# Query and key halves copied by transfers, stick-breaking sums over summed later blocks, bias rows on GpSimd, in a two-layer hybrid trunk

## Chip, cores and metric

One core of a Trainium2 chip runs the whole kernel in one launch. The metric is the device time in microseconds of one execution.

## What is computed

Input x is 512 tokens of 1024 values, float32. Each of 2 layers has a SwiGLU feed-forward part (inner width 2816), a mixer of three causal attention branches, and a second feed-forward part; a last norm closes. The mixer, shortened from the reference:

```python
u = _rmsnorm(h, mix_norm[l])
z = u @ w_in[l]
(a_q, a_k, a_v, b_q, b_k, b_v, b_f, c_q, c_k, c_v, g) = jnp.split(z, split_idx, axis=-1)
...
# branch A: softmax(q k + ALiBi), two of them, p[0] - lam * p[1]; 4 heads of 2 x 64
# branch B: softmax(q k + c_q - c_k), c = cumsum(log_sigmoid(forget)); 8 heads of 64
# branch C, stick-breaking, 8 heads of 64:
z = jnp.einsum('bqhd,bkhd->bhqk', qb, k).astype(f32) * scale
log_keep = jnp.where(strict, jax.nn.log_sigmoid(-z), 0.0)
later = lax.cumsum(log_keep, axis=3, reverse=True) - log_keep
w = jnp.where(strict, jnp.exp(jax.nn.log_sigmoid(z) + later), 0.0)
...
m = (gates[:, :, 0] * (o_a @ proj_a[l]) + gates[:, :, 1] * (o_b @ proj_b[l]) + gates[:, :, 2] * (o_c @ proj_c[l]))
h = h + m @ w_out[l]
```

What matters below is `later`: for each key, the sum of the log factors over all keys that come after it.

## The kernel before

Everything is kept transposed: features on the 128 partitions, the 512 tokens along the row. Products run in a rounded 32-bit format. To keep float32 accuracy a value is held as two parts, a high part (ACT rounds, helper `hi`, line 755) and a low part (DVE subtracts, helper `lo`, line 1098), and a product is three matmuls (`three`, lines 372 to 374): high x high, high x low, low x high.

**Weights** come as a stream of units: one unit is 128 x 1024 values, eight blocks, 512 KB. SyncE (SP) loads unit n + 3 into the slot of unit n as soon as DVE has made unit n's low part (`w_set`); three slots. `split(k)` on ACT and on DVE makes the two parts of slot k. One unit through PE is 24 matmuls of 512 columns (`u_unit`).

**The head tiles.** In the mixer a layer has 4 tiles, each with 128 columns of every branch: two heads of B, two of C, one of A (with its two softmaxes). One tile takes 9 units of w_in (`HEAD_UNITS`): q, k, v for C, then B, then A. Unit n's product lies in PSUM bank n mod 2; DVE takes it (`take`, line 1208), scaled by the norm, to `tile(n % 2)` and counts `staged`. PE works through a written-out order (`heads` and `rest_of_tile`): between blocks of units (`unit(4, 0, 3)` is blocks 0 to 2 of unit 4) it puts scores, transposes (`turn_values`, `turn_probs`), sums and weighted products of the heads, so that ACT and DVE have time to prepare them. ACT and DVE have their own written-out orders for the same work; each engine runs strictly in its order and waits on semaphores. `rest_of_tile` finishes branch A of the tile before, while the units of the next one begin. The first tile of a layer also has the forget gate (`forget`) in it.

**Query and key halves.** A q or k unit holds two heads, 64 partitions each. `qk_hi` on ACT writes rounded halves where the score matmuls want them: q of each head twice (`q_twice`), k once (`k_both`), and for branches A and B once more (`k_bias`), each from the half in `tile`: 4, 2 or 4 operations of 64 x 512. `qk_lo` on DVE writes the low halves: 2 of 64 x 512. The other halves of `q_rest` hold bias rows (`rows`, DVE, line 1228), 4 in a tile, that select the head's forget or ALiBi bias from `bias_l`.

**Stick-breaking.** The 4 key blocks of 128 keys have their own PSUM banks (`SB0 + j`), with the queries from block j on: 512, 384, 256 and 128 columns. `stick_scores` fills them, block 0 first. ACT makes log(1 + exp(-|z|)) in three operations for each block (`stick_logs`), DVE completes it (`stick_softplus`), and both split it into parts in `PT_HI` and `PT_LO`. `stick_sums` then adds to bank j a triangular product of block j and a product with a matrix of -1 for each later block i:

```python
for i in range(NQ):
    pe.wait_ge(pt_set, c.next(pt_set))
    n, *parts = wide_keys(i)
    for j in range(i + 1):
```

`wide_keys` gives at least 256 columns; for block 3, zeros stand beside its 128. The banks are then exponentiated (`stick_exp`), split (`stick_hi`, `stick_lo`) and multiplied with the values (`weighted(2, hd)`), which waits for the low part of one block after the other.

## Time and profile before

| | |
|---|---|
| median of 3 runs | 2586.7 us (2586.26 to 2587.92) |
| the profiled execution | 2585.08 us, its span 2583.3 us |
| PE busy | 2554.5 us, 99% |
| DVE busy | 1429.1 us, 55% |
| ACT busy | 1119.4 us, 43% |
| granted clock of PE, mean | 0.998 |
| one head tile | 76.9 us, 8 of them |
| moved by DMA | 238 MB, mean 92 GB/s |

All times are microseconds from the span's start. PE, ACT, DVE, POOL (GpSimd) and SP (SyncE) are the engines. L372 is line 372 of the kernel. Matmuls are pipelined and their ends are modelled, so the pitch of their starts tells more than their duration. An idle time in a row stands in brackets with the work that ended it.

### The profile page before, as it was taken

The numbers are of one execution on the slowest core, as the hardware profiler recorded it, in microseconds if no ns is written. First come the engines' busy times: TensorE is split into PE (matmuls) and PEld (weight loads), VectorE is DVE, ScalarE is ACT, GpSimd is POOL, SyncE is SP. The second block draws the span as 40 slices with busy tenths as digits, with TensorE's granted clock in tenths as the row PEclk, the third lists the DMA queues.
The fourth block names the chain that finished last, engine by engine and source line by source line (L and its number), as shares of the span: only waits on it lengthen the run. The fifth ranks groups of instructions, "written<-read, shape, count | busy, mean of one in ns | idle before, by whom it ended". The sixth has DMA issues, their size and how long they took to land.

```text
span 2583.3 us, 36860 instructions
## 1 busy us (share of the span) xinstructions
PE 2554.5 (99%) x11838; PEld 2124.9 (82%) x11838; DVE 1429.1 (55%) x2164; ACT 1119.4 (43%) x1888; POOL 3.5 (0%) x12
## 2 busy tenths in 40 slices
PE   7999999999999999999999999999999999999997
PEld 6888888888888888888888888888888888888886
DVE  5444347888854454444344443488888455544434
ACT  4223237777732242232232222478776223422322
POOL 0000000000000000000000000000000000000000
PEclk9999999999999999999999999999999999999999
DMA  4222332111222232223332223221212322322233
GB/s 168 97 97 95 101 106 66 59 66 58 66 95 94 88 123 98 97 94 102 106 107 97 97 94 102 97 67 58 66 58 66 103 93 96 115 97 96 94 104 105
DMA packets 65767, 238.05 MB, mean 92 GB/s; under 512 B 7296, under 2 KB 7552, under 8 KB 65408
## 3 DMA queue, kind: packets, MB, share of 16 engines
q1 hardware_dynamic: 65664, 236.79, 27.6%
q8 instruction: 52, 0.85, 0.1%
q14 instruction: 51, 0.42, 0.1%
HBM read 234.66 MB, written 2.10 MB: 92 GB/s over the span
## 4 chain that ended last, share of the span: by engine, by line
PE 97%; DVE 1%; issue 1%; ACT 0%; DMA 0%; DVEq 0%; ACTq 0%; SPq 0%
PE ps L372 30%; PE ps L374 30%; PE ps L373 30%; PE ps L529 2%; PE ps L460 1%; PE ps L449 1%; PE ps L503 1%; PE ps L502 1%; PE ps L451 1%; PE ps L516 0%; PE ps L466 0%; PE ps L518 0%; DVE scratch L1114 0%; PE ps L445 0%; PE ps L536 0%
## 5 line engine op out<-in xcount | busy, mean ns | idle before, releaser
L755 ACT ACTIVATE w_hi<-w_raw 128x1024 fp32r<-128x1024 f32 x441 | 468.4, 1062 | 1164.2 <-PE ps L374 1163.4
L372 PE MATMUL ps<-u_hi,w_hi 128*128 128x512 f32 x2368 | 929.1, 392 | 11.3 <-DVE w_lo L1098 11.3
L374 PE MATMUL ps<-u_hi,w_lo 128*128 128x512 f32 x2368 | 922.9, 390 | 0.0
L373 PE MATMUL ps<-u_lo,w_hi 128*128 128x512 f32 x2368 | 922.7, 390 | 0.0
L1098 DVE TENSOR_TENSOR w_lo<-w_raw,w_hi 128x1024 fp32r<-128x1024 f32 x441 | 538.2, 1222 | 313.3 <-ACT w_hi L755 305.8
L372 PEld LDWEIGHTS ps<-u_hi,w_hi 128*128 128x128 f32 x2368 | 445.4, 188 | 103.2 <-issue 12.3
L374 PEld LDWEIGHTS ps<-u_hi,w_lo 128*128 128x128 f32 x2368 | 445.1, 188 | 93.8
L373 PEld LDWEIGHTS ps<-u_lo,w_hi 128*128 128x128 f32 x2368 | 445.4, 188 | 90.8 <-issue 1.2
L372 PE MATMUL ps<-area,w_hi 128*128 128x512 f32 x1024 | 398.8, 389 | 0.4 <-DVE h L1118 0.4
L374 PE MATMUL ps<-area,w_lo 128*128 128x512 f32 x1024 | 398.4, 389 | 0.0
L373 PE MATMUL ps<-area,w_hi 128*128 128x512 f32 x1024 | 398.4, 389 | 0.0
L755 ACT ACTIVATE area<-scratch 64x512 fp32r<-64x512 f32 (+5 forms) x426 | 235.4, 583 | 123.7 <-DVE scratch L1449 64.0
L1098 DVE TENSOR_TENSOR area<-scratch,area 128x512 f32 (+5 forms) x336 | 199.2, 611 | 56.0 <-ACT area L755 53.1
L372 PEld LDWEIGHTS ps<-area,w_hi 128*128 128x128 f32 x1024 | 192.2, 188 | 42.1 <-issue 2.5
L374 PEld LDWEIGHTS ps<-area,w_lo 128*128 128x128 f32 x1024 | 192.2, 188 | 40.0
L373 PEld LDWEIGHTS ps<-area,w_hi 128*128 128x128 f32 x1024 | 192.2, 188 | 39.9
L1132 DVE TENSOR_TENSOR scratch<-ps,rstd 128x512 f32<-128x512 f32 x88 | 60.9, 692 | 257.0 <-PE ps L374 257.0
L1128 DVE TENSOR_TENSOR scratch<-ps,rstd 128x512 f32<-128x512 f32 x88 | 60.9, 692 | 187.4 <-PE ps L374 179.0
L1430 DVE TENSOR_TENSOR scratch<-ps,rstd 128x512 f32<-128x512 f32 x48 | 33.0, 690 | 100.6 <-PE ps L374 100.4
L845 ACT ACTIVATE scratch<-ps,stat 128x128 f32<-128x128 f32 (+3 forms) x128 | 66.2, 524 | 34.3 <-DVE stat L1233 34.3
L1108 DVE SCALAR_TENSOR_TENSOR u_lo<-h,par,u_hi (+1 forms) x56 | 41.6, 751 | 63.7 <-ACT u_hi L767 63.7
L1118 DVE SCALAR_TENSOR_TENSOR h<-ps,h 128x512 f32 (+1 forms) x48 | 33.1, 691 | 67.9 <-PE ps L374 67.9
(118 smaller groups left out, 1563.2 us busy)
## 6 DMA issues: line engine op xcount, KB each, us to landing
w_raw<-weights SPq DMA_DIRECT2D x441, 512.0 KB, 3.3
h<-x SPq DMA_DIRECT2D x2, 1024.0 KB, 6.7
out<-scratch SPq DMA_DIRECT2D x8, 256.0 KB, 2.2
scratch<-const_b SPq DMA_DIRECT2D x1, 512.0 KB, 10.5
scratch<-const_r SPq DMA_DIRECT2D x1, 320.0 KB, 9.7
scratch<-lambdas SPq DMA_DIRECT2D x1, 256.0 KB, 10.7
cst<-const SPq DMA_DIRECT2D x1, 137.0 KB, 3.1
par<-params SPq DMA_DIRECT2D x1, 94.0 KB, 2.1
```

What stands on the lines that cost most here:

```text
L372: pe.matmul(dst, hi, x_hi, start=start, stop=False, **kw)
L373: pe.matmul(dst, hi, x_lo, start=False, stop=False, **kw)
L374: return pe.matmul(dst, lo, x_hi, start=False, stop=stop, **kw)
L529: last = pe.matmul(ps[:, SB0 + j, width - n:width], negtri_r if i == j else negones_r, part, start=False, stop=i == NQ - 1, skip_group_che ...
L755: return act.activation(dst, src, ACT.Copy)
L845: act.activation(query_block(buf, i), ps[:, SB0 + i, 0:(i + 1) * P], ACT.Exp, bias=neg_max(buf, i), accum_out=total(buf, i)).then_inc(exp_ ...
L1098: return dve.tensor_tensor(dst, src, hi_part.bitcast(F32), ALU.subtract)
L1108: dve.scalar_tensor_tensor(u_lo[:, bass.ds(at, SEQ)], h[:, bass.ds(at, SEQ)], times(gain), u_hi[:, bass.ds(at, SEQ)].bitcast(F32), ALU.mul ...
L1118: dve.scalar_tensor_tensor(h[:, bass.ds(at, SEQ)], ps[:, bank, :], factor, h[:, bass.ds(at, SEQ)], ALU.mult, ALU.add).then_inc(h_set, 1)
L1128: dve.tensor_tensor(a, ps[:, 2 * pair, :], rstd[:], ALU.mult).then_inc(gate_in, 1)
L1132: dve.tensor_tensor(b, ps[:, 2 * pair + 1, :], rstd[:], ALU.mult).then_inc(up_set, 1)
L1430: dve.tensor_tensor(tile(6 * (k % 2)), ps[:, k, :], rstd[:], ALU.mult).then_inc(tail_read, 1)
```

## The change

Six things change together, all in the mixer.

1. **Transfers copy the halves.** `qk_hi` becomes one rounding of 128 x 512 into one new tile `rounded`, and `qk_lo` one subtraction in place in `tile(k % 2)`. SP issues transfers of 64 x 512 (128 KB) from there to `q_twice`, `k_both`, `k_bias` and `q_rest`: 22 for high parts and 12 for low parts in a tile. They stand in SP's one queue between the weight loads, in a written-out order (`tile_loads`). ACT may round the next one only when the last high parts have landed and DVE has read `rounded`; `take` may overwrite `tile(k % 2)` only when its low parts have landed; the first scores of a branch wait for all of it (`wait_qk`).
2. **Sums over summed blocks.** Key blocks are scored and worked on in the order 3, 2, 1, 0. DVE adds block 3 to block 2 and the result to block 1 (`later_sum`), the sums are split (`later_hi`, `later_lo`) into a new area, and `stick_sums` has 14 matmuls for 20. Each bank counts `stick_set` when it is complete, so ACT may exponentiate bank 3 first. `weighted(2, hd)` waits for all four blocks.
3. **Bias rows on GpSimd.** The four `rows` of a tile run there, let go by the fourth take of the tile.
4. **Base rows** of the bias are loaded again in each layer, in float32, straight into `bias_l` and `tile(6)`; the copies at the start go away, and so do four tiles (`o_rest`, `o_whole`, `base_l`, `base_r`). `o_whole` is now `tile(7)`. In the first tile of a layer, both bias tiles are finished ahead of the take of k.
5. **PE's order** is shifted by one to three blocks at most places: values and probabilities are turned earlier, the sums of both heads start one block later.
6. **The orders of ACT and DVE** are rewritten to fit.

```diff
+            def move_hi(branch, which):
+
+                sp.wait_ge(qk_hi_set, counts.next(qk_hi_set))
+                for hd in range(2):
+                    src = rounded[half(hd), :].bitcast(F32)
+                    if which == 0:
+                        sp.dma_start(q_twice(branch, hd)[half(hd), :].bitcast(F32), src).then_inc(hi_moved, 16)
+                        sp.dma_start(q_twice(branch, hd)[half(1 - hd), :].bitcast(F32), src).then_inc(hi_moved, 16)
+                    else:
+                        sp.dma_start(k_both(branch, hd)[half(hd), :].bitcast(F32), src).then_inc(hi_moved, 16)
+                        if branch != 2:
+                            sp.dma_start(k_bias(branch, hd)[half(hd), :].bitcast(F32), src).then_inc(hi_moved, 16)
+
+            def move_lo(branch, which, k):
+
+                sp.wait_ge(qk_lo_set, counts.next(qk_lo_set))
+                for hd in range(2):
+                    src = tile(k % 2)[half(hd), :]
+                    dst = q_rest(branch, hd)[half(hd), :] if which == 0 else k_both(branch, hd)[half(1 - hd), :]
+                    sp.dma_start(dst.bitcast(F32), src).then_inc(lo_moved[k % 2], 16)
+
+            def tile_loads(base):
+
+                load_next(base, 0)
+                move_hi(2, 0)
+                move_lo(2, 0, 0)
+                move_hi(2, 1)
+                move_lo(2, 1, 1)
+                load_next(base + 1, 1)
+                load_next(base + 2, 2)
+                move_hi(1, 0)
+                move_lo(1, 0, 3)
+                load_next(base + 3, 0)
+                move_lo(1, 1, 4)
+                move_hi(1, 1)
+                load_next(base + 4, 1)
+                load_next(base + 5, 2)
+                load_next(base + 6, 0)
+                move_hi(0, 0)
+                move_lo(0, 0, 6)
+                move_lo(0, 1, 7)
+                move_hi(0, 1)
+                load_next(base + 7, 1)
+                load_next(base + 8, 2)
+
...
+                def rows(head, branch, hd):
+                    o = half(1 - hd)
+                    pool.tensor_scalar(q_rest(branch, hd)[o, :], bias_l[o, :], cst[o, C_SEL + head:C_SEL + head + 1], None,
+                                       ALU.mult).then_inc(rows_set, 1)
+
+                pool.wait_ge(bias_set, layer + 1)
+                for t in range(NT):
+
+                    pool.wait_ge(staged, (layer * NT + t) * HEAD_UNITS + 4)
+                    rows(2 * t, 1, 0)
+                    rows(2 * t + 1, 1, 1)
+                    rows(t + N_FOX, 0, 0)
+                    rows(t + N_FOX, 0, 1)
...
+            def wait_qk(branch):
+
+
+                pe.wait_ge(hi_moved, c.next(hi_moved, 16 * (6 if branch == 2 else 8)))
+                for k in range(2):
+                    pe.wait_ge(lo_moved[k], c.next(lo_moved[k], 16 * 2))
...
+                if branch == 2:
+                    pe.wait_ge(pt_set, c.next(pt_set, NQ))
                 for j in range(NQ):
-                    pe.wait_ge(pt_set, c.next(pt_set))
+                    if branch != 2:
+                        pe.wait_ge(pt_set, c.next(pt_set))
...
-                for j in range(NQ):
+                for j in reversed(range(NQ)):
...
             def stick_sums():
 
-                for i in range(NQ):
+                def add(j, matrix, parts, m, stop):
+                    n = max(WIDE, (NQ - j) * P)
+                    for k, part in enumerate(parts):
+                        last = pe.matmul(ps[:, SB0 + j, n - m:n], matrix, part, start=False, stop=stop and k == 1,
+                                         skip_group_check=True)
+                    return last
+
+                def own(j, stop):
                     pe.wait_ge(pt_set, c.next(pt_set))
-                    n, *parts = wide_keys(i)
-                    for j in range(i + 1):
-                        width = max(WIDE, (NQ - j) * P)
-                        for part in parts:
-                            last = pe.matmul(ps[:, SB0 + j, width - n:width], negtri_r if i == j else negones_r,
-                                             part, start=False, stop=i == NQ - 1, skip_group_check=True)
-                        if i == NQ - 1:
-                            last.then_inc(stick_set, 1)
+                    n, *parts = wide_keys(j)
+                    return add(j, negtri_r, parts, n, stop)
+
+                def all_later(j, stop):
+                    pe.wait_ge(pt_set, c.next(pt_set))
+                    parts = later(LATER_HI, j), later(LATER_LO, j)
+                    return add(j, negones_r, parts, (NQ - 1 - j) * P, stop)
+
+
+
+                own(3, True).then_inc(stick_set, 1)
+                own(2, False)
+                n, *parts = wide_keys(3)
+                add(2, negones_r, parts, n, True).then_inc(stick_set, 1)
+                own(1, False)
+                all_later(1, True).then_inc(stick_set, 1)
+                all_later(0, False)
+                own(0, True).then_inc(stick_set, 1)
...
             def heads(before):
 
                 if before:
                     rest_of_tile(unit)
-                    unit(2)
+                    unit(2, 0, 5)
                     turn_probs(0)
-                    unit(3, 0, 3)
+                    unit(2, 5)
                     weighted_whole()
-                    unit(3, 3, 5)
+                    unit(3, 0, 4)
                     diff_norm()
+                    unit(3, 4, 5)
                 else:
                     unit(0, first=True, before=False)
                     sum_of_squares()
@@ -582,26 +705,25 @@
                 unit(4, 0, 3)
                 if before:
                     pe.wait_ge(o_rstd, c.next(o_rstd))
-                unit(4, 3, 6)
                 turn_values(0)
+                unit(4, 3, 7)
                 stick_sums()
-                unit(4, 6)
+                unit(4, 7)
                 unit(5, 0, 4)
                 weighted(2, 0, before)
                 stick_scores(1)
                 unit(5, 4)
-                unit(6, 0, 7)
+                unit(6)
                 stick_sums()
-                unit(6, 7)
-                unit(7, 0, 4)
+                unit(7, 0, 2)
+                turn_values(1)
+                unit(7, 2, 4)
                 weighted(2, 1)
                 scores(1, 0)
-                unit(7, 4, 5)
-                turn_values(1)
-                unit(7, 5)
-                unit(8, 0, 1)
+                unit(7, 4)
+                unit(8, 0, 2)
                 turn_probs(0)
-                unit(8, 1)
+                unit(8, 2)
                 weighted(1, 0)
                 scores(1, 1)
                 c.skip(exp_set, 2 * NQ)
...
             def qk_hi(branch, which, k, takes=1):
                 act.wait_ge(staged, c.next(staged, takes))
-                for hd in range(2):
-                    src = tile(k % 2)[half(hd), :]
-                    if which == 0:
-                        hi(q_twice(branch, hd)[half(1 - hd), :], src)
-                        last = hi(q_twice(branch, hd)[half(hd), :], src)
-                    else:
-                        last = hi(k_both(branch, hd)[half(hd), :], src)
-                        if branch != 2:
-                            last = hi(k_bias(branch, hd)[half(hd), :], src)
-                last.then_inc(qk_hi_set, 1)
+
+                act.wait_ge(hi_moved, c.value(hi_moved))
+                act.wait_ge(qk_lo_set, c.value(qk_lo_set))
+                hi(rounded[:], tile(k % 2)).then_inc(qk_hi_set, 1)
+                c.skip(hi_moved, 16 * (2 if branch == 2 and which else 4))
+                c.skip(qk_lo_set)
...
+            def later_hi(j):
+                act.wait_ge(later_sum_set, c.next(later_sum_set))
+                hi(later(LATER_HI, j), key_block(1, j + 1)).then_inc(pt_hi_set, 1)
...
+                softplus_hi(3)
+                softplus_hi(2)
+                softplus_hi(1)
+                values_hi(2)
+                later_hi(1)
+                split(0)
+                later_hi(0)
                 softplus_hi(0)
-                softplus_hi(1)
-                softplus_hi(2)
-                split(0)
-                softplus_hi(3)
-                values_hi(2)
+                stick_exp(3)
+                stick_exp(2)
                 if before:
                     output_hi(0, t - 1)
+                stick_exp(1)
                 stick_exp(0)
-                stick_exp(1)
-                stick_exp(2)
-                stick_exp(3)
+                stick_hi(3)
+                stick_hi(2)
+                stick_hi(1)
                 stick_hi(0)
                 split(1)
-                stick_hi(1)
-                stick_hi(2)
-                stick_hi(3)
                 qk_hi(1, 0, 3, 2)
+                output_rest(0)
                 stick_logs(0)
...
+                dve.wait_ge(base_landed, layer * 32 + 32)
+                dve.scalar_tensor_tensor(bias_l[:], run_hi, mask(0), bias_l[:], ALU.mult, ALU.add).then_inc(vec_done, 1)
                 dve.wait_ge(vec_done, c.next(vec_done))
-                dve.scalar_tensor_tensor(bias_l[:], soft, mask(1), bias_l[:], ALU.mult, ALU.add).then_inc(vec_done, 1)
+                dve.scalar_tensor_tensor(bias_l[:], soft, mask(1), bias_l[:], ALU.mult, ALU.add).then_inc(bias_set, 1)
+                dve.scalar_tensor_tensor(right, run_hi, mask(2), right, ALU.mult, ALU.add).then_inc(vec_done, 1)
                 dve.wait_ge(vec_done, c.next(vec_done))
-                stage(1, 1.0)
-                dve.scalar_tensor_tensor(neg, run_hi, mask(2), base_r[:], ALU.mult, ALU.add).then_inc(vec_done, 1)
-                dve.wait_ge(vec_done, c.next(vec_done))
-                dve.scalar_tensor_tensor(neg, soft, mask(3), neg, ALU.mult, ALU.add).then_inc(forget_in, 1)
-                c.skip(forget_in)
-
-            def stage(k, scale):
-                take(k, scale)
-                split(k % SLOTS)
+                dve.scalar_tensor_tensor(right, soft, mask(3), right, ALU.mult, ALU.add).then_inc(forget_in, 1)
+                take(1, 1.0)
+                split(1)
...
             def take(k, scale):
 
-                if k >= 2:
-                    dve.wait_ge(qk_set, c.peek(qk_set, 0))
+
+                dve.wait_ge(lo_moved[k % 2], c.value(lo_moved[k % 2]))
                 dve.wait_ge(unit_done, c.next(unit_done))
                 dve.scalar_tensor_tensor(tile(k % 2), ps[:, k % 2, :], scale, rstd[:], ALU.mult, ALU.mult
                                          ).then_inc(staged, 1)
 
-            def stage_qk(branch, which, k):
-                stage(k, SCALE if which == 0 else 1.0)
-                qk_lo(branch, which, k)
-
             def qk_lo(branch, which, k):
                 dve.wait_ge(qk_hi_set, c.next(qk_hi_set))
-                for hd in range(2):
-                    src = tile(k % 2)[half(hd), :]
-                    if which == 0:
-                        last = lo(q_rest(branch, hd)[half(hd), :], src, q_twice(branch, hd)[half(hd), :])
-                    else:
-                        last = lo(k_both(branch, hd)[half(1 - hd), :], src, k_both(branch, hd)[half(hd), :])
-                last.then_inc(qk_set, 1)
-                c.skip(qk_set)
-
-            def rows(head, branch, hd):
-                o = half(1 - hd)
-                dve.tensor_scalar(q_rest(branch, hd)[o, :], bias_l[o, :], cst[o, bass.ds(head + C_SEL, 1)], None,
-                                  ALU.mult).then_inc(rows_set, 1)
+                lo(tile(k % 2).bitcast(F32R), tile(k % 2), rounded[:]).then_inc(qk_lo_set, 1)
+                c.skip(lo_moved[k % 2], 16 * 2)
...
+            def later_sum(j):
+
+                k = key_block(1, j + 1)[:, P:]
+
+                dve.wait_ge(pt_set, c.value(pt_set))
+                dve.tensor_tensor(k, k, key_block(1, j + 2), ALU.add).then_inc(later_sum_set, 1)
+
+            def later_lo(j):
+                dve.wait_ge(pt_hi_set, c.next(pt_hi_set))
+                lo(later(LATER_LO, j), key_block(1, j + 1), later(LATER_HI, j)).then_inc(pt_set, 1)
...
+                stick_softplus(3)
+                take(3, SCALE)
+                stick_softplus(2)
+                stick_softplus(1)
                 stick_softplus(0)
-                stick_softplus(1)
-                stick_softplus(2)
-                stick_softplus(3)
+                softplus_lo(3)
+                softplus_lo(2)
+                later_sum(1)
+                softplus_lo(1)
+                later_lo(1)
+                later_sum(0)
+                later_lo(0)
                 softplus_lo(0)
-                softplus_lo(1)
-                softplus_lo(2)
-                softplus_lo(3)
                 if before:
                     output_lo(0, t - 1, layer)
-                take(3, SCALE)
                 values_lo(2)
+                stick_lo(3)
+                stick_lo(2)
+                stick_lo(1)
                 stick_lo(0)
+                take(4, 1.0)
+                qk_lo(1, 0, 3)
+                split(0)
+                output_whole(0)
+                split(1)
+                stick_softplus(3)
+                stick_softplus(2)
+                stick_softplus(1)
+                stick_softplus(0)
+                softplus_lo(3)
+                softplus_lo(2)
+                later_sum(1)
+                softplus_lo(1)
...
```

## Rows read from the trace of the kernel before

**Rows 1.** the page: its span and the busy time of the engines.
```profile
span 2583.3 us, 36860 instructions
...
PE 2554.5 (99%) x11838; PEld 2124.9 (82%) x11838; DVE 1429.1 (55%) x2164; ACT 1119.4 (43%) x1888; POOL 3.5 (0%) x12
```

**Rows 2.** waits of PE over the span: total us, times, longest.
```profile
PE ps L372 <- DVE w_lo L1098: 11.3, 2, 10.7
PE ps L393 <- DVE scratch L1114: 6.8, 2, 3.5
```

**Rows 3.** a stage of the trace, one tile: busy us and count by engine.
```profile
504.00:581.00 77.00, 77.00 (x418) 65.89 (x417) 64.48 (x136) 60.46 (x139) 0.00 (x0) 1.00 0.19 63
```

**Rows 4.** timeline of PE, pitch of matmuls by width: start us, us.
```profile
497.05 0.39 PE L502 MATMUL ps<-area,v_area 128*128 128x512 f32 x1
497.28 0.39 PE L503 MATMUL ps<-area,v_area 128*128 128x512 f32 x1
497.51 0.33 PE L502 MATMUL ps<-area,v_area 128*128 128x384 f32 x1
...
497.85 0.28 PE L502 MATMUL ps<-area,v_area 128*128 128x256 f32 x1
497.97 0.28 PE L503 MATMUL ps<-area,v_area 128*128 128x256 f32 x1
```

**Rows 5.** timeline of PE in the tile of 529 to 606.
```profile
558.90 0.39 PE L512 MATMUL ps<-cst_b 128*128 128x128 bf16 x4
...
560.47 0.40 PE L372 MATMUL ps<-u_hi,w_hi 128*128 128x512 f32 x1
...
566.97 3.06 PE L529 MATMUL ps<-area,cst_r 128*128 128x512 f32 x20
569.87 0.40 PE L372 MATMUL ps<-u_hi,w_hi 128*128 128x512 f32 x1
...
573.97 0.39 PE L502 MATMUL ps<-area,v_area 128*128 128x512 f32 x1
```

**Rows 6.** ACT by form, 504 to 581: busy, mean ns.
```profile
L755 ACT ACTIVATE area<-scratch 64x512 fp32r<-64x512 f32 x22 | 13.4, 627 | 0.3
```

**Rows 7.** DVE by form, 504 to 581: busy, mean ns.
```profile
L1098 DVE TENSOR_TENSOR area<-scratch,area 64x512 fp32r<-64x512 f32 x12 | 8.2, 686 | 0.5 <-ACT area L755 0.3
...
L1228 DVE TENSOR_SCALAR area<-bias_l,cst 64x512 fp32r<-64x512 f32 x4 | 1.9, 481 | 0.1
```

**Rows 8.** timeline of ACT in that tile, logarithms and roundings.
```profile
560.37 0.96 ACT L857 ACTIVATE scratch<-ps 128x512 f32<-128x512 f32 x2
...
564.52 1.36 ACT L755 ACTIVATE area<-scratch 128x512 fp32r<-128x512 f32 x3
```

**Rows 9.** timeline of DVE in that tile.
```profile
549.93 0.75 DVE L1253 SCALAR_TENSOR_TENSOR scratch<-scratch,stat 128x512 f32<-128x512 f32 x1
...
555.08 2.79 DVE L1098 TENSOR_TENSOR area<-scratch,area 64x512 fp32r<-64x512 f32 x4
...
565.19 1.50 DVE L1098 TENSOR_TENSOR area<-scratch,area 128x512 fp32r<-128x512 f32 x3
...
567.26 0.75 DVE L1291 SCALAR_TENSOR_TENSOR scratch<-ps,lam,scratch 128x512 f32<-128x512 f32 x1
```

**Rows 10.** DMA issues on SP's queue at the start: start us, us.
```profile
4.85 0.45 SPq L334 DMA_DIRECT2D scratch<-const_b  x1
```

**Rows 11.** DMA issues by line: KB each, us to landing.
```profile
w_raw<-weights SPq DMA_DIRECT2D x441, 512.0 KB, 3.3
...
out<-scratch SPq DMA_DIRECT2D x8, 256.0 KB, 2.2
```

**Rows 12.** timeline of PE and DVE in the first tile of layer 0.
```profile
401.52 0.75 DVE L1196 SCALAR_TENSOR_TENSOR scratch<-scratch,cst 128x512 f32<-128x512 f32 x1
...
405.05 0.40 PE L512 MATMUL ps<-cst_b 128*128 128x128 bf16 x4
```

**Rows 13.** one source line on POOL: ns min/median/max.
```profile
L355 POOL MEMSET area<- x2: 521/524/526, 391.0 to 1666.4; 64x512 f32 x2
```

247 lines of the change are left out of this document (137 added, 110 removed).

## The prediction

> **What bounds the kernel now.** I read the page first: TensorE (PE) is busy for 2554.5 of 2583.3 us, VectorE (DVE) for 1429, ScalarE (ACT) for 1119 [rows 1]. A busy PE can still be a waiting PE, so the next view is the waits of PE: 11.3 and 6.8 us, in two places each, at the start and around the norms, and nothing in the mixer [rows 2]. The stage view of one head tile (77 us) says the same: PE 77.00, DVE 64.5, ACT 60.5 [rows 3]. So inside a tile PE never starves, and only two things can move the time: matmul work that goes away, and a wait that appears. Work taken from ACT and DVE is worth nothing by itself; it buys slack. The last view is the timeline of PE, for the price of a matmul: 512 columns start 0.23 us apart (0.227 over long runs), 384 columns 0.17, 256 columns 0.12 [rows 4].
>
> **The matmuls that go.** `stick_sums` runs 16 times (2 layers, 4 tiles, 2 heads). Before, key block i goes through the matrix unit once for each block j <= i, in a high and a low part: 2 matmuls of 512 columns, 4 of 384, 6 and 8 of 256. By the pitches that is 2 x 0.23 + 4 x 0.17 + 14 x 0.12 = 2.82 us; the trace has 2.90 from the first of the 20 to the next matmul, the changeover from the transposes included [rows 5]. After: own blocks 3, 2, 1, 0 (256, 256, 384, 512 columns), block 3 into bank 2 (256), the summed blocks into bank 1 (256) and bank 0 (384), each twice: 8 of 256, 4 of 384, 2 of 512, 2.10 us. Six of 256 columns are gone: 6 x 0.118 = 0.71 us, 16 times: **11.3 us**. No other matmul changes its shape or count; the moved transposes and blocks are the same ones in another order, so I price the move at nothing on PE itself. What can hold it back are the operands.
>
> **Work off PE.** Per tile ACT drops 22 half-tile roundings of 627 ns (13.4 us) [rows 6] and gains 6 full ones of about 0.64 and 4 of the summed blocks (0.4 to 0.5 each): some 7.8 us less. DVE drops 12 half-tile subtractions of 686 ns and 4 bias rows of 481 ns [rows 7], gains 6 subtractions of 0.69 and 8 small ones for the sums: some 3 us less. PE hides both engines, so they are worth 0. Dropped with them is one 512 KB constant at the start, behind the loads that matter: 0.
>
> **The first sum of a tile, followed step by step.** Times are those of the profiled tile. The first-head scores start at 558.90 and end at 560.47, the sums start at 566.97 [rows 5]. ACT takes 4.15 us from the first absolute value to the first rounding (560.37 to 564.52) [rows 8]. In the new order the norm of branch A is 0.68 us (three matmuls) earlier and block 3, the narrow one, is scored first, so ACT starts at about 559.7 and rounds from 563.8. Then comes a ladder between DVE and ACT that was not there: round blocks 3, 2, 1; their low parts; sum of 2 and 3 (ready 565.7); ACT rounds it to 566.2; its low part 566.65; sum with block 1 at 567.1; ACT rounds it (384 columns) to 567.65 and block 0 to 568.2; low part of block 0 ready at 568.95. The durations of the steps are those of the same widths: 1.50 us for low parts of 512, 384 and 256 columns together [rows 9], 1.36 for the roundings [rows 8]. The 1.06 us rounding of weights in the middle is under the ladder's DVE steps. PE starts the sums one block later, at 567.65, and reaches block 0 last, 12 matmuls or 1.64 us on: 569.3. Slack 0.35 us: no wait, but little to spare. The second head has no such squeeze: PE puts 36 matmuls (8.2 us) there, and I find 1.4 us of slack.
>
> **The weighted product behind it** now waits for all four blocks at once, since they come in the order 3 to 0. Sums end 569.75, 15 matmuls later PE is there: 573.2 (573.97 before, [rows 5]). DVE from the low part of block 0, at pitches of 0.6 to 0.65 [rows 9]: output of branch A (0.65), ACT rounds it (0.7), its low part (0.6), values (0.7), low parts of 3, 2, 1 (0.95) and 0 (0.7): 573.3. I charge 0.15 us in the 6 tiles that have a tile before: **+0.9**.
>
> **The transfers.** SP takes 0.45 us for one issue [rows 10], and a transfer lands 2.2 us (256 KB out) to 3.3 us (512 KB weights) after it [rows 11]. The line through the two gives 1.65 us for the 128 KB of a half; nothing in the trace copies SBUF to SBUF, so I bound it by 1.65 and 3.3 and take 2.2, the nearest row. The Trainium skill (DMA: Bandwidth & Descriptors, Anatomy of one DMA) gives some 2.0 us plus bytes by 436 GB/s, 2.3 us here, for another issue path; by that the sum would be the same. The tight place is branch C's keys. The last difference and the take of k's unit end at 550.68 now [rows 9]; the scores in front of them come three matmuls (0.68 us) earlier, so 550.0, in the other order. ACT rounds q by 550.6; four issues, the last started at 551.9 and landed at 554.1. Today DVE starts on q's low part at 555.08 [rows 9]; the transposes ahead of it move up by 9 matmuls (2.0 us), the 1.2 us of a weight remainder is in the way, and I put its end at 554.0. Only after both may ACT round k: 554.8. Two issues for its high parts, two for the low parts, the last started at 556.2, landed at 558.4. The scores start at 558.90: no wait. In the first tile of a layer the left and right bias come ahead of k; the bias ends about where it does now, 402.27, k's low part at 402.7, the last issue starts at 403.15 and lands at 405.35, and PE is there at 405.05 [rows 12]: 0.3 us, twice: **+0.6**. On SP the weight loads stand behind these waits: the load behind branch B's moves comes some 10 us later than its slot is free, but lands (3.3 us) some 7 us before its rounding. The others have more. Transfers of the other branches have 1 us or more to spare; they are used a head later.
>
> **Bias rows on GpSimd.** Four 64x512 products per tile, let go by the fourth take, at about 563.5. DVE does one in 0.48 us [rows 7]; on GpSimd the trace has only a fill of that shape, 0.52 us [rows 13], as the lower end; as the upper, 1.1 us, twice it. They end between 565.7 and 568, and nobody needs them before 590. But from 564.75 DVE is on the ladder. If the two engines get in each other's way, DVE is late by d, and the product behind the ladder by nearly all of it (6 tiles), the sums of the first tiles by d less 0.35. No row shows them together; below, d = 0; above, each of the last two or three GpSimd operations holds DVE for its length, d = 2 or more. I take d = 0.3, half of one operation, since a DVE operation there is short and half the rows are done by then: 6 x 0.3 = **+1.8**.
>
> The Trainium skill (SBUF, Who interferes with whom) says a DVE instruction with two SBUF inputs and a GpSimd one that reads SBUF exclude each other for the whole instruction. No trace here shows it. It is rival B.
>
> **Sum.** -11.3 + 0.9 + 0.6 + 1.8 = -8.0 us. The profiled execution took 2585.08 us (span 2583.3), 1.6 under the median of the runs; its span would become 2575.3, and the median 2586.7 - 8.0 = **2578.7 us**.
>
> **Rivals.**
> - A, the above, 50%. Its own range: 2575.4 with no wait at all, to 2581.5.
> - B, GpSimd holds DVE, 25%. For: the rows start 1.2 us ahead of the ladder and last at least 2.1. Against: the last two-input operations of DVE may fit between. With d = 1.2: -11.3 + 1.5 + 6 x 1.2 + 2 x 0.85 = -0.9, **2585.8**. Up to d = 0.65 it stays faster by 0.2%.
> - C, the transfers are late, 20%; this is the one that ends slower. The chain holds two landings in a row, since q and k share one rounded tile. With a landing of L us the last one is at 553.98 + 2L in the 6 later tiles, and at 403.15 + L in the 2 first. L = 3.3, as weights take: 1.7 x 6 + 1.4 x 2 = 13 in place of A's 0.6: +4.4, **2591**. It costs the gain from L = 2.6, and makes the kernel slower by 0.2% from 3.4; at L = 4, some **2601**. For: 64-partition copies are not in the trace, and issues of 0.45 us follow each other. Against: 256 KB took 2.2.
> - D, the sums give nothing, because a wait that PE's modelled ends hide sits there already: 5%, **2586.7**. Against: the 20 matmuls run at the pitch of their widths.
>
> **Chances.** A change of 0.2% (5.2 us) is about what a measurement of this kernel can tell from none. Faster: all of A and parts of B and C (d up to 0.65, L up to 2.6): 0.60. Same: the middle of B and C, and D: 0.24. Slower: C from L = 3.4, B from d = 2.0: 0.16. The range reaches from no waits and a little more, 2574.5, to near C's 2591, 2590, with some 5% left out below and 13% above.
>
> **What would show it.** In the profile after: 14 matmuls per sum, 2.1 us from the first to the next, and PE without named waits except about 0.3 us at the first scores of a layer. B shows as two-input DVE operations in the ladder longer than 0.69 us or starting late while POOL is busy, and a wait of PE for the low parts of the first head. C shows as PE waiting for a DMA at the branch C scores, and as a time to landing above 2.6 us. I am wrong if the tile does not get 1.42 us shorter but for these waits, or if a wait shows in the second head or in branches A and B, whose chains I found loose.

## The result

The changed kernel takes 2595.75 us (median of 7 runs, 2594.02 to 2598.28); the kernel before took 2586.7 us beside it (7 runs, 2585.55 to 2587.92). The ratio is 1.0035, 95% interval 1.0023 to 1.0046: slower by 9 us, where I had predicted 8 us faster and a range that ended at 2590.0. The profiled execution took 2594.02 us.

The page of the changed kernel, to be read beside [rows 1]:

```profile
span 2592.2 us, 37391 instructions
...
PE 2551.0 (98%) x11742; PEld 2111.8 (81%) x11742; DVE 1414.4 (55%) x2146; ACT 1055.3 (41%) x1792; POOL 56.8 (2%) x44
```

TensorE is busy for 3.5 us less, ACT for 64 and DVE for 15 less, and the span is 8.9 us longer: work went and waits came. The waits of PE name them (engine, output, line of the waiting instruction, what it waited for: total us, times, longest):

```profile
PE ps L467 <- DVE w_lo L1236: 13.0, 2, 10.7
PE ps L488 <- DVE scratch L1252: 5.9, 2, 3.5
PE ps L617 <- DMA area<-scratch: 3.9, 8, 0.7
PE ps L631 <- DVE area L1236: 3.9, 8, 0.5
PE ps L547 <- DMA area<-rounded: 1.7, 7, 0.3
PE ps L607 <- DVE area L1236: 1.3, 6, 0.2
PE ps L467 <- issue: 0.8, 1, 0.8
```

The first two are those of [rows 2]. The next four are new, once for each tile or nearly: branch C's scores (L617) and B's (L547) wait for a transfer, the first sums of a tile (L631) and the weighted product behind them (L607) for DVE. The last is a single stop at 1297.7, where layer 1 begins. The named part of such a wait is less than what PE loses, since the ends of matmuls are modelled; the loss is the gap less the pitch of a matmul. The timeline of PE in one tile (start us, busy us, engine, line) shows both kinds:

```profile
482.72 0.40 PE L469 MATMUL ps<-u_hi,w_lo 128*128 128x512 f32 x1
483.83 0.40 PE L617 MATMUL ps<-cst_b 128*128 128x128 bf16 x4 [0.71 <-DMA area<-scratch]
...
492.73 1.88 PE L631 MATMUL ps<-area,cst_r 128*128 128x256 f32 x12
495.09 0.73 PE L631 MATMUL ps<-area,cst_r 128*128 128x512 f32 x2 [0.48 <-DVE area L1236]
495.65 0.39 PE L467 MATMUL ps<-u_hi,w_hi 128*128 128x512 f32 x1
...
498.83 0.39 PE L469 MATMUL ps<-u_hi,w_lo 128*128 128x512 f32 x1
499.44 0.50 PE L607 MATMUL ps<-area,v_area 128*128 128x512 f32 x1 [0.22 <-DVE area L1236]
```

The 14 matmuls of the first sums last from 492.73 to 495.65, 2.92 us, against 2.90 for the 20 of before [rows 5]; the second head's last 2.10 against 2.81. So the shorter sums are there, and the first ones lose all of it to one wait, for the low part of block 0. From the start of one tile's first sums to the next it is 77.9 us (492.73 to 570.62), against 76.92 before (490.05 to 566.97). By the same view of both kernels, piece by piece: first sums +0.02, second -0.71, C's scores +0.5, the product behind the sums +0.5, B's scores +0.4, and +0.2 at changeovers from transposes to matmuls, of which a tile has one or two more; +0.9 of the 1.0. Both layers show it alike. Outside the mixer one place differs: where layer 1 begins, PE's step from the last matmul to the next is 1.14 us and was 0.39. The trace names nothing that PE waits for there. Every variant below with the transfers has such a stop, 0.8 to 1.6 us beyond the pitch; (3) and (4), without them, have 0.2 and 0.4, as the kernel before has 0.2.

What holds DVE in the ladder is seen where its timeline is read against GpSimd's (POOL). First DVE, the ladder of the first head and behind the dots the same steps of the second; then POOL:

```profile
488.28 1.48 DVE L1388 SCALAR_TENSOR_TENSOR scratch<-ps,scratch 128x256 f32<-128x256 f32 x3
489.67 0.62 DVE L1236 TENSOR_TENSOR area<-scratch,area 128x128 fp32r<-128x128 f32 x2
490.32 0.67 DVE L1400 TENSOR_TENSOR scratch<-scratch 128x128 f32<-128x128 f32 x1
490.91 0.99 DVE L1236 TENSOR_TENSOR area<-scratch,area 128x384 fp32r<-128x384 f32 x2
491.93 0.85 DVE L1400 TENSOR_TENSOR scratch<-scratch 128x256 f32<-128x256 f32 x1
493.37 1.66 DVE L1236 TENSOR_TENSOR area<-scratch,area 128x384 fp32r<-128x384 f32 x2 [0.59 <-ACT area L879]
...
507.32 0.29 DVE L1400 TENSOR_TENSOR scratch<-scratch 128x128 f32<-128x128 f32 x1
507.53 1.00 DVE L1236 TENSOR_TENSOR area<-scratch,area 128x384 fp32r<-128x384 f32 x2
508.56 0.42 DVE L1400 TENSOR_TENSOR scratch<-scratch 128x256 f32<-128x256 f32 x1
509.58 1.22 DVE L1236 TENSOR_TENSOR area<-scratch,area 128x384 fp32r<-128x384 f32 x2 [0.59 <-ACT area L879]
```

```profile
488.46 6.91 POOL L446 TENSOR_SCALAR area<-bias_l,cst 64x512 fp32r<-64x512 f32 x4 [70.84 <-DVE scratch L1344]
```

Four bias rows take GpSimd 6.91 us, 1.7 each, where I had 1.1 as the upper bound. Beside them three steps of DVE that read SBUF twice (two tensor inputs there) are longer: 0.67 for 0.29, 0.85 for 0.42, 1.66 for 1.22 us (two steps in one row), in all 1.25. The steps between them, and those with an input from PSUM (L1388), keep their time.

Narrower windows give the merged rows one by one, and show where in a GpSimd instruction the hold lies:

```profile
490.12 1.60 POOL L446 TENSOR_SCALAR area<-bias_l,cst 64x512 fp32r<-64x512 f32 x1
490.32 0.67 DVE L1400 TENSOR_TENSOR scratch<-scratch 128x128 f32<-128x128 f32 x1
493.48 1.89 POOL L446 TENSOR_SCALAR area<-bias_l,cst 64x512 fp32r<-64x512 f32 x1
493.90 1.13 DVE L1236 TENSOR_TENSOR area<-scratch,area 128x512 fp32r<-128x512 f32 x1
```

In all 8 tiles the held steps are the 24 that start 0.11 to 0.42 us after a bias row's start; each is 0.37 to 0.45 us longer. Those that start 0.75 us or more after it keep their time, though the row runs 1.57 us. Where a DVE step was already running at a row's start, that step keeps its time, and in the fourth row of each tile the row is the longer one, 1.89 us.

Last, SP's queue ahead of branch C's scores (an issue, its us):

```profile
473.20 0.47 SPq L367 DMA_DIRECT2D area<-rounded  x1
473.71 0.59 SPq L368 DMA_DIRECT2D area<-rounded  x1
474.35 0.59 SPq L367 DMA_DIRECT2D area<-rounded  x1
...
478.15 1.10 SPq L380 DMA_DIRECT2D area<-scratch  x2
479.36 1.36 SPq L370 DMA_DIRECT2D area<-rounded  x2
480.83 1.17 SPq L380 DMA_DIRECT2D area<-scratch  x2
```

An issue of a 64-partition copy holds SP for 0.6 us, at a pitch of 0.64, not 0.45 as the load of [rows 10]. The last one starts at 481.4 and PE goes on at 483.83. The median time to landing is as predicted:

```profile
area<-rounded SPq DMA_DIRECT2D x176, 128.0 KB, 2.3
area<-scratch SPq DMA_DIRECT2D x96, 128.0 KB, 2.3
```

### The profile page after: what moved, and what is told of

It is laid out like the page before. It is cut to its first block, busy times and chain, and to the rows that moved or that the text cites. A ratio compares the mean times of both kernels' runs of the same rounds, so it can differ in the third digit from the quotient of the medians.

```text
span 2592.2 us, 37391 instructions
## 1 busy us (share of the span) xinstructions
PE 2551.0 (98%) x11742; PEld 2111.8 (81%) x11742; DVE 1414.4 (55%) x2146; ACT 1055.3 (41%) x1792; POOL 56.8 (2%) x44
## 4 chain that ended last, share of the span: by engine, by line
PE 86%; DVE 5%; issue 3%; ACT 2%; DMA 1%; SPq 1%; DVEq 0%; ACTq 0%
PE ps L467 27%; PE ps L469 27%; PE ps L468 27%; DVE area L1236 2%; PE ps L562 1%; PE ps L551 1%; PE ps L607 1%; DMA area<-scratch 1%; PE ps L553 1%; PE ps L608 1%; SPq L380 1%; ACT area L879 1%; SPq L370 1%; DMA area<-rounded 0%; DVE scratch L1400 0%
## 5 line engine op out<-in xcount | busy, mean ns | idle before, releaser
L879 ACT ACTIVATE area<-scratch 128x512 f32 (+5 forms) x298 | 151.9, 544 | 150.4 <-DVE scratch L1589 64.4
L1236 DVE TENSOR_TENSOR area<-scratch,area 128x512 f32 (+4 forms) x288 | 165.9, 589 | 46.2 <-ACT area L879 45.8
```

What stands on the lines that cost most here:

```text
L879: return act.activation(dst, src, ACT.Copy)
L1236: return dve.tensor_tensor(dst, src, hi_part.bitcast(F32), ALU.subtract)
```

## The experiments

Each was timed in 5 rounds with the kernel before beside it (2586.1 to 2586.3 us on these chips), ratios with 95% intervals. My theory was that two rivals of the prediction had come true together: B (GpSimd holds DVE) and C (transfers late, by their issues, not by their landing). Against it stood: the lateness is DVE's own order, and the bias rows anywhere would give the same.

**1. Bias rows back on DVE**, in the places that they had before; all else as changed.

```
+                take(5, 1.0)
+                qk_lo(1, 2, 4)
+                rows(t * 2, 1, 0)
...
                 take(7, 1.0)
+                rows(t * 2 + 1, 1, 1)
...
                 split(2)
+                rows(t + N_FOX, 0, 0)
+                rows(t + N_FOX, 0, 1)
```

> The changed kernel with the four bias rows of a tile back on DVE (two in the second head, two at the tile's end); transfers and sums as changed. Theory 1 (the GpSimd operations hold DVE in the first ladder: in the changed kernel the first sums take 2.94 us for 2.09, and PE waits another 0.53 us at the product behind them): 8 tiles x about 1.3 us come back, 2595.75 - 10.5 = 2585 us, the first sums take 2.1 to 2.2 us. Rival (the ladder itself is too long, GpSimd only stands beside it; and DVE now has 1.9 us more in a tile): no gain, 2594 to 2597, the first sums stay near 2.9 us.

**2. Bias rows on GpSimd, a take later**: its wait on `staged` is for 5 instead of 4, so the rows start behind the ladder of the first head.

> The changed kernel, the rows still on GpSimd but let go by the fifth take of the tile instead of the fourth, behind the first head's ladder. Theory 1: the ladder is free of it, the first sums take 2.1 us and about 10 us come back, 2585 to 2587, unless the 6.6 us of GpSimd reach into the second head's ladder, which has 1.4 us to spare. If it is GpSimd reading SBUF at all times that slows the core, not the place: no gain, 2595. Rival of the ladder being too long by itself: 2594 to 2597.

Measured: (1) 2587.91 us, ratio 1.0008 (0.9999 to 1.0017); (2) 2589.72, 1.0015 (1.0006 to 1.0024). In both the first sums last 2.10 us and PE has no wait for DVE there. So GpSimd beside the ladder cost 7.8 us by (1), and either cure works for the sums. (2) pays elsewhere: PE's named waits at B's scores are 4.9 us, against 1.9 in (1). What is left in (1), against the kernel before, is the transfers' part:

```profile
PE ps L603 <- DMA area<-scratch: 3.9, 8, 0.6
PE ps L533 <- DMA area<-rounded: 1.9, 8, 0.3
```

**3 and 4. No transfers at all**: ACT and DVE write every half themselves, as before the change, but in the changed kernel's orders; rows on GpSimd (3) and on DVE (4).

```
-                hi(rounded[:], tile(k % 2)).then_inc(qk_hi_set, 1)
+                for hd in range(2):
+                    src = tile(k % 2)[half(hd), :]
+                    if which == 0:
+                        hi(q_twice(branch, hd)[half(1 - hd), :], src)
+                        last = hi(q_twice(branch, hd)[half(hd), :], src)
...
```

> The changed kernel, but ACT and DVE write the halves of q and k themselves as before, and no transfers for them; rows on GpSimd and the new sums stay. Theory 1 (transfers cost 0.55 to 0.9 us at the first scores of branch C in a tile and 0.4 us at those of branch B, some 8 us in all): 2595.75 - 8 = 2588 us, and no wait of PE at either place. Rival (ACT and DVE need the time the transfers freed): their 7 and 3 us a tile come back as waits in the ladders, 2595 or more.

> Both undone: halves written by ACT and DVE, rows on DVE. What stays of the change is the sums over summed blocks and the new orders. Theory 1: the gain of the sums, 16 x 0.71 = 11.3 us less about 1 us of small waits, shows alone: 2576 to 2577 us, all sums at 2.1 us. Rival (the sums need the room that transfers and GpSimd make): ladder too long, 2582 or more. If the two costs do not add, x1 and x3 together do not give this one's gain over the changed kernel.

Measured: (3) 2629.61 us, 1.0160 (1.0146 to 1.0174); (4) 2623.39, 1.0143 (1.0127 to 1.0158). They miss by 42 and 47 us. The bias rows on GpSimd cost 6.2 us here too. PE no longer waits at the scores of C and B; it waits at the weighted products of B and A. The rows of (4), with those of (3) nearly the same:

```profile
PE ps L551 <- DVE area L1179: 19.8, 19, 1.3
...
PE ps L551 <- DVE v_area L1179: 8.3, 8, 1.1
```

So the changed orders can't carry the half roundings: where a full rounding stands now, up to four of a half stand ahead of the values and turned probabilities (the transposed ones, in their two parts) that PE needs next. Taking work off ACT and DVE was worth something after all: the new orders spend it. Whether the halves with the old orders of those branches would keep the sums' gain wasn't tried.

**5. B's high key parts issued before its low ones** on SP, from (1). **6. C's low key halves written by DVE**, two half operations in place of one full and two transfers, from (1). **7. Both.**

```
-                move_lo(1, 1, 4)
                 move_hi(1, 1)
+                move_lo(1, 1, 4)
...
-                move_lo(2, 1, 1)
...
+                if branch == 2 and which:
+                    for hd in range(2):
+                        last = lo(k_both(branch, hd)[half(1 - hd), :], tile(k % 2)[half(hd), :], rounded[half(hd), :])
```

> The kernel with the rows on DVE (2587.9 us), and for branch B's k SP issues the four high transfers ahead of the two low ones. In that kernel's trace an issue of 64 partitions holds SP for 0.6 us, the low ones come first, and PE waits 0.40 us in every tile at the first scores of B, until the last high one has landed. Theory (the wait is the sum of the issues behind the later of two events): the high ones start 1.4 us earlier, the last landing of the six is 0.6 to 0.9 us earlier, the wait goes: 8 x 0.4 = 3.2 us, 2584.7 us. Rival (the landing time grows when transfers crowd, whatever their order): 2587.9, wait unchanged.

> The kernel with the rows on DVE (2587.9 us), but the low halves of branch C's k are written by DVE in two half operations (0.69 us more of DVE) and not by transfers. The last transfer in front of the first scores of C is then one of k's high halves, issued 1.4 us earlier. Theory: PE's wait there (0.6 us in six tiles, 0.7 to 1.0 in the first of a layer) goes, or is held to 0.1: 4 to 5 us, 2583 us. Rival (the first landing in the chain, q's, or DVE's own lateness sets it): 2587 or more.

> Both edits of the two kernels above together, rows on DVE. Theory: the two waits are in different places and add: 3.2 + 4.5 = 7.7 us off 2587.9, 2580 us, faster than the kernel before by 0.2%. What is then left of the sums' 11.3 us is lost to small waits at the weighted products. If they do not add: 2583 or more.

Measured: (5) 2589.63 us, 1.0014 (1.0005 to 1.0023), no gain: B's wait is gone, 3.1 us by the gaps, and 1.7 us in 6 places stand by name at the product with the turned probabilities of B's second head. By the gaps it is 2.4 us more there than in (1), and 2.4 more at the transposes of the first head's. (6) 2584.0 us, 0.9992 (0.9983 to 1.0001): C's wait is all but gone, 3.9 us won. (7) 2584.84, 0.9994 (0.9985 to 1.0003): B's part again gives nothing. In (5) and (7) the wait moves on; the row of (7):

```profile
PE ps L597 <- DVE area L1227: 1.7, 6, 0.3
```

By DVE's timeline of (7) two bias rows (1.0 us) and the take of a unit (0.67) stand there ahead of the low parts for which PE waits.

**8. The old sums**, 20 matmuls and no summed blocks, from (1).

> The kernel with the rows on DVE (2587.9 us), but the sums as before: every later block multiplied by itself, 20 matmuls for 14, in the new order 3, 2, 1, 0, and the additions and splits of summed blocks left out. Same result. Theory (six matmuls of 256 columns are 0.71 us of PE, 16 times, and in this kernel both sums run without a wait): 11.4 us more, 2599 us. Rival (the ladder of the summed blocks costs as much as it saves, or the matmuls left out were hidden): 2588 to 2594.

Measured: 2602.7 us, 1.0066 (1.0052 to 1.0080), 14.8 over (1). The sums last 2.83 us each; 16 x 0.73 is 11.7, and the waits at C's scores grow from 3.9 to 6.3 us. The price of the matmuls is right; the waits at C's scores and a little more make the rest.

**9. Orders tidied**, from (7): three bias rows together into a gap of 1.2 us that DVE has ahead of the second head's low parts; the take of a unit behind the turned probabilities; and the low part of a weight slot (`split(0)` on DVE, a weight remainder for short, 1.2 us) moved behind the seventh take.

```
                 rows(t * 2, 1, 0)
+                rows(t * 2 + 1, 1, 1)
+                rows(t + N_FOX, 0, 0)
...
-                split(0)
                 output_whole(1)
...
                 take(7, 1.0)
-                rows(t * 2 + 1, 1, 1)
+                split(0)
+                rows(t + N_FOX, 0, 1)
```

> The kernel with bias rows on VectorE, C's low key halves written by VectorE and B's high key parts issued first (it ran 2584.8), with three steps of VectorE's order moved: the bias rows of B (both) and A (one) stand together in the gap of 1.2 us ahead of the second head's low parts, the fourth row and one weight remainder behind the seventh take, and the first take of a unit behind the last low part of the turned probabilities. Left out: nothing. Theory (every wait of a tile is VectorE's order, so moving the late work into its idle time removes it): the product behind the turned probabilities of head 1 of branch B loses its wait of 0.66 us, the turned probabilities of the head before lose 0.21; 8 and 8 times, -6.5 us: 2578.3 us, faster than the kernel before by 0.3%. Rival (each removed wait returns at the next order, as when the low and the high parts were swapped): 2584 to 2586.

Measured: 2625.07 us, 1.0148 (1.0134 to 1.0162), 40 us over (7). One wait makes most of it, at the product of B's first head (the rest is told in the last section):

```profile
PE ps L597 <- DVE area L1227: 30.0, 8, 4.1
```

SP's queue, of (7) and then of (9), shows the way. The load of weights into slot 0 stands ahead of the transfers of A's queries (L367) and waits for the remainder that I had moved; SP takes its queue in order. The transfers left at 526.06 and not 519.60, where PE in (9) is 4.7 us later (the turned probabilities of B's first head start at 524.08 and not 519.41): 1.8 us late, and now right behind 512 KB of weights. ACT, which rounds A's keys after them, went on 3.9 us after their last issue and not 2.4, and the product waits behind it:

```profile
511.05 5.09 SPq L352 DMA_DIRECT2D w_raw<-weights  x3
519.60 0.47 SPq L367 DMA_DIRECT2D area<-rounded  x1
```

```profile
515.71 10.24 SPq L352 DMA_DIRECT2D w_raw<-weights  x3
526.06 0.47 SPq L367 DMA_DIRECT2D area<-rounded  x1
```

**10. GpSimd fills beside the ladder**, from (1): twelve fills of 64x512 in the place of the bias rows, which DVE still makes later.

```
+                    pool.wait_ge(staged, (layer * NT + t) * HEAD_UNITS + 4)
+                    for n in range(12):
...
+                        pool.memset(q_rest(branch, hd)[half(1 - hd), :].bitcast(F32), 0.0).then_inc(filled, 1)
```

> The kernel with bias rows on VectorE (2587.9), and in addition GpSimd fills the same four half tiles with zeros, three times over, let go by the fourth take as the bias rows were (12 fills of 64x512, about 0.52 us each and so some 6.3 us beside the ladder; VectorE writes the bias rows over them later). Theory (GpSimd holds VectorE where it reads SBUF; a fill reads nothing): two-input operations of the ladder keep 0.29 and 0.42 us, first sums 2.10 us, 2587.9. Rival (any GpSimd instruction of that stretch holds VectorE by some 0.4 us, by its start or its writes): sums at 2.9 us or more, and 2594 to 2600.

**11. The changed kernel, bias rows in eight instructions of 64x256; 14. in sixteen of 64x128.** The same elements.

```
+                    for n in range(2):
+                        at = slice(n * SEQ // 2, (n + 1) * SEQ // 2)
+                        last = pool.tensor_scalar(q_rest(branch, hd)[o, at], bias_l[o, at],
```

> The changed kernel (2595.8) with each bias row of 64x512 on GpSimd made in two of 64x256, eight instructions a tile for the same elements. Theory 1 (VectorE loses about 0.4 us at each GpSimd instruction that it meets, whatever its length): the ladder meets six or more in place of three, first sums 3.7 us or more in place of 2.94, 2601 to 2606. Theory 2 (VectorE loses a share of the time in which GpSimd reads): the same elements, the same loss, sums 2.9 us, 2595 to 2597.

> The changed kernel with each bias row in four instructions of 64x128, sixteen a tile, for the same elements. Measured so far: with 4 instructions of 1.7 us VectorE's two-input operations lose about 0.4 us at each, with 8 of 1.1 us about 0.1. Theory (the loss belongs to the length of one instruction, VectorE is held only while a long one runs on): no loss at all in the ladder, operations at 0.29 and 0.42 us, first sums 2.10, 2588 us. Rival (a fixed loss of some 0.1 us at each start has been hidden by the few starts): the ladder meets twice as many as with eight, and the time is 2591 or more.

Measured: (10) 2588.04 us, 1.0005 (0.9996 to 1.0014), as (1). The fills ran 6.84 us beside the ladder, as long as the bias rows, and DVE's steps kept 0.29 and 0.43 us:

```profile
488.01 6.84 POOL L452 MEMSET area<- 64x512 f32 x12 [70.26 <-DVE scratch L1339]
```

So it is not GpSimd's running, its starts or its writes. (11) 2589.61 us, 1.0014 (1.0005 to 1.0023), and (14) 2588.87, 1.0008 (0.9999 to 1.0017): 6 to 7 us under the changed kernel. Both theories of (11) missed: the loss at one GpSimd instruction shrinks with its length. DVE in the ladder of (11), where POOL was busy for 8.6 us:

```profile
489.61 0.29 DVE L1403 TENSOR_TENSOR scratch<-scratch 128x128 f32<-128x128 f32 x1
...
490.94 0.43 DVE L1403 TENSOR_TENSOR scratch<-scratch 128x256 f32<-128x256 f32 x1
491.96 1.45 DVE L1239 TENSOR_TENSOR area<-scratch,area 128x384 fp32r<-128x384 f32 x2 [0.59 <-ACT area L882]
```

The last pair there is still 0.23 us long; in (14) it takes 1.23. Over the whole traces, against the same steps away from GpSimd, DVE steps with two SBUF inputs that run beside a bias row are longer (by more than 0.06 us) in 24 of 64 cases in the changed kernel, 9.8 us in all; in 26 of 88 in (11), at most 0.24 each and 3.8 in all; in 16 of 126 in (14), at most 0.10 each and 1.2 in all. Beside the fills of (10) none of 70 is, and no DVE step of another kind in any of them. A fill lasts only 0.52 us, but a 64x128 piece of (14) alone lasts 0.60 and still costs a little, so length alone does not explain it.

The hold goes the other way too, and there it is long. In (14) the 26 pieces with no such DVE step beside them took 0.59 to 0.61 us; all 16 that met a weight remainder (two SBUF inputs, 1.2 us) took 1.83 to 1.88:

```profile
501.80 1.83 POOL L448 TENSOR_SCALAR area<-bias_l,cst 64x128 fp32r<-64x128 f32 x1
501.95 1.21 DVE L1239 TENSOR_TENSOR w_lo<-w_raw,w_hi 128x1024 fp32r<-128x1024 f32 x1
```

**12. The order of (9) without the moved remainder. 13. Rows in eight pieces on GpSimd**, with the changes of (7) and the later take.

> The tidied order without the one step that moved a weight remainder: bias rows of B (both) and A (one) together in VectorE's gap ahead of the second head's low parts, the fourth where B's second row was, the first take of a unit behind the last low part of the turned probabilities. Left out: nothing. Theory (the 3.6 us wait of the tidied order came from SP alone: it stood in order at the weight load that waits for the moved remainder, with branch A's transfers behind it): no wait at the product of B's first head, and the 0.66 us wait at the turned probabilities of its second head gone: 2584.8 - 8 x 0.66 = 2579.5 us. Rival (the regrouped rows or the later take are what held it): 2600 or more, with the wait still there.

> The changed kernel with the bias rows on GpSimd in eight instructions of 64x256 (2589.6), C's low key halves written by VectorE, B's high key parts issued first, and the first take of a unit behind the turned probabilities. Left out: nothing. Theory (waits of TensorE add up and VectorE has no rows to make, so nothing takes their place): C's wait of 0.5 to 0.8 us and B's of 0.4 go, 8 times each: some 2582 us. Rival (the rows in pieces still cost the ladder some 0.4 us a tile and VectorE's extra half operation at C eats the rest): 2586 to 2589.

Measured: (12) 2582.31 us, 0.9984 (0.9975 to 0.9993), where I expected 2579.5. The 30 us of waits are gone, so the moved remainder was their cause; that it acted through SP's queue is what (15) tests. (7)'s wait at the product of B's second head is gone too. What remains is at the transposes of B's first head's probabilities, some 2.8 us in 8 tiles, with two weight remainders ahead on DVE. (13) 2584.84, 0.9995 (0.9986 to 1.0004): the waits for transfers go, but 0.4 us a tile stay in the ladder and behind it.

**15. The remainder moved after all, and SP's queue with it**, from (12): `split(0)` behind the fourth bias row, and the high transfers of A's queries ahead of the load that waits for it.

```
-                load_next(base + 6, 0)
                 move_hi(0, 0)
+                load_next(base + 6, 0)
...
-                split(0)
                 output_whole(1)
...
                 rows(t + N_FOX, 0, 1)
+                split(0)
```

> The kernel of the mended order (2582.3), which still shows TensorE waiting 0.22 to 0.49 us a tile for the turned probabilities of B's first head, whose last share VectorE makes at the end of a row of steps with two weight remainders in front. Here one of the two (slot 0, 1.2 us) goes behind the fourth bias row, and on SP the four high transfers of A's queries stand ahead of the weight load that waits for it, so that the queue doesn't stop as it did in the tidied order. Left out: nothing. Theory: that wait goes, 8 x 0.35 = 2.8 us, and nothing takes its place (A's key rounding waits for its transfers till then anyway): 2579.5 us, faster than the kernel before by 0.26%. Rival (A's key halves or the turned probabilities behind them become the wait): 2581 to 2585, with a wait at the product of B's first head.

Measured: 2578.35 us, ratio 0.9971 (0.9960 to 0.9983), 17.4 us under the changed kernel and 7.9 under the kernel before. With the queue reordered the moved remainder costs nothing, and the 2.8 us of (12) are gone. In the mixer's tiles no named wait of PE is left; one tile in its stage view (us, then busy us and count of PE, PEld, DVE, ACT, POOL, then the granted clock):

```profile
490.20:566.00 75.80, 75.80 (x405) 64.23 (x404) 64.02 (x139) 52.28 (x127) 0.00 (x0) 1.00 0.43 119
```

## Why the prediction was wrong

Two terms failed, by about as much: the bias rows on GpSimd (the choice of d and its bounds, +1.8 us for 7.8), and the transfers (the issues on SP, +0.6 for 8.3 by the gaps in the trace, of which (6) gave back 3.9 in the time).

- **The matmuls that go**: right. 14 matmuls take 2.09 to 2.10 us, 0.71 less than 20, and (8) against (1) confirms it in the time. The change as made did not keep it.
- **The ladder**: right in its slack. DVE lost 1.25 us in it, less the 0.35 us of slack 0.9, and the sums wait 0.8. In (1), without GpSimd, they don't wait. Those of the second head don't in either, as predicted.
- **Bias rows on GpSimd, d = 0.3, +1.8 us**: this is the term that was mis-sized, 7.8 us by (1). The upper bound of 1.1 us was twice a fill [rows 13]. A fill reads nothing, so it bounded neither the length (1.7 us measured) nor what the reading does to DVE. I also charged d to the product only, but the first sums of all 8 tiles pay it. As rival B had it, two-input steps were longer while POOL was busy, with d = 1.25. Its price for d = 1.2, 6 x 1.2 for the product and 2 x 0.85 for the sums, is 8.9 us, and the trace has 8.9 too, but by luck: 0.73 x 8 = 5.9 at the sums of all tiles and 0.5 x 6 = 3.0 at the product. The Trainium skill (SBUF — State Buffer, Who interferes with whom) says that a DVE instruction with two SBUF inputs contends with a GpSimd one that reads SBUF, not with one that only writes it. The traces agree on who: (10) shows no loss, L1388 with its PSUM input none. On how long they differ, in one direction, from the hold for the whole instruction that the prediction drew from it: a DVE step lost 0.4 us to a GpSimd instruction of 1.57. In the other direction they agree: in (14) a GpSimd piece lost 1.2 us to a DVE step of 1.2.
- **The transfers, +0.6 us**: the landing was right (2.3 us for 2.2), and so rival C in its form (L from 2.6) did not come. The wait is there all the same, 0.53 to 0.88 us at C's scores of every tile, 5.2 us in all, and in the first tile of a layer 0.7 for the 0.3 that I had. I took 0.45 us for an issue from a 128-partition load [rows 10], and counted four issues behind ACT's rounding of the keys, as if SP were free. It was not: the two low transfers of the queries (1.10 us) stand there first, and the four behind them go at 0.64. From the end of ACT's rounding (478.8) to the last issue it is 2.6 us, not 1.4. That is 1.2 us more, and landing 0.2; had it been 1.4 us, the last part would have landed ahead of PE. (6), which drops two of these issues, all but removes the wait.
- **"1 us or more to spare" in the other branches**: wrong. B's scores waited 0.30 to 0.43 us in every tile, 3.1 us in all, for the last of the high key parts, which stood behind the low ones: (5) turned the two around and that wait went, without gain in the time.
- **The product behind the sums, +0.9**: right as far as (1) shows it; there 0.12 us in each of the 6 tiles stay, with GpSimd 0.5.
- **Work off ACT and DVE is worth 0**: it left out that the change's new orders spend it. With the work put back under these orders, (3) is 34 us slower than the changed kernel and (4) 35 us slower than (1).

The range failed since each rival was priced with the others held still. B and C both came, and their waits stand in different places, so they add up. By the gaps of the changed kernel's trace, each less the pitch of its matmul: -11.3 for the matmuls, +5.9 at the first sums, +3.0 at the product behind them, +5.2 at C's scores, +3.1 at B's, +1.3 for changeovers, +0.8 at the start of layer 1; that is +8.0 of the 8.9 by which the span grew. The rest is spread over places too small to name.

What stays open: why a GpSimd instruction of 512 columns holds DVE by 0.4 us, one of 256 by 0.1 to 0.2 and one of 128 by 0.1 at most, and what PE does in the stop at the start of layer 1. The fills of (10) do no arithmetic and read nothing, so the runs alone do not say which of the two matters; no run here parts them.

## What to carry to other kernels

Before an operation moves to an idle engine, ask for a row of that engine with the same reads; a fill is no bound for a product. Walk every queue past which something moves, by position: on SP an issue of 0.6 us and a load that waits for another engine both hold back everything behind them, and one reordered remainder cost 40 us until the queue was reordered with it. When matmuls go, the gain is only kept if the chains that were hidden by a fraction of a microsecond are shortened too: here it took five small edits of places and orders to keep 7.9 us of the 11.3, and in (5) and (7) a wait that was removed showed up again one step on.

## What the runs showed that I had not expected

A wait of PE can cost more than itself. In (9) PE stood still for 3.6 us, and behind it the granted clock was lower, near 0.5 of the 2.4 GHz (its 1.2 GHz level) for some 4 us (stage, us, busy us and count by engine, then the granted clock):

```profile
529.40:534.00 4.60, 1.30 (x8) 0.91 (x7) 1.52 (x4) 0.80 (x2) 0.00 (x0) 1.00 0.47 109
534.00:536.00 2.00, 2.00 (x14) 1.96 (x13) 1.96 (x4) 0.34 (x2) 0.00 (x0) 0.63 0.77 177
536.00:538.00 2.00, 2.00 (x7) 1.52 (x6) 1.63 (x3) 1.91 (x7) 0.00 (x0) 0.52 0.88 203
538.00:540.00 2.00, 2.00 (x10) 1.60 (x9) 1.89 (x8) 1.66 (x4) 0.00 (x0) 1.00 0.80 257
```

The scores there took 0.97 us more than their 1.37 and the 12 matmuls behind them 0.6 more: 3.6 + 1.6 = 5.2 us a tile, 8 times that is 42, for the 40 measured. Waits of 0.5 to 0.8 us, as in the changed kernel, left the clock at 1.00 over the tile. And GpSimd's pace is not that of its elements alone: the shortest bias row took 1.56 us for 64x512, 0.92 for 64x256 and 0.59 for 64x128, about 0.3 us and 0.3 more for every 128 columns. The averages beside DVE are longer, 1.7, 1.0 and 0.9, since DVE holds it as well.
